# Token groups of 400, 256 and 400, with a joined 512-column matmul for the middle one

## Chip, cores and metric

The kernel runs on one core of a Trainium2 chip. The metric is the device time of one execution in microseconds (us).

## What is computed

One step of a two-layer encoder trunk over 1056 tokens (1024 of a prompt, 32 of a running stream), width 1024, in fp32 accuracy. Layer 0 mixes tokens with a gated width-3 convolution, layer 1 with trailing means over 2, 4, 8 and 16 frames. Each mixer is followed by a squared-ReLU MLP with 4096 hidden features.

```python
def short_conv_mixer(x, hist, w_in, conv_w, w_out):
    gb, gc, h = jnp.split(x @ w_in, 3, axis=-1)
    u = gc * h
    ...
    y = (gb * conv) @ w_out
...
        h = layer_norm(ALPHA * x + y, ln1_g[i], ln1_b[i])
        r = jax.nn.relu(h @ mlp_w1[i])
        f = (r * r) @ mlp_w2[i]
        e = (p[i] @ ple_w[i]) * jax.nn.sigmoid(h @ ple_gate_w[i])
        x = layer_norm(ALPHA * h + f + e, ln2_g[i], ln2_b[i])
```

## The kernel before

Features lie on the 128 partitions and tokens along the free dimension. A feature block is 128 features, so width 1024 is KD = 8 blocks and a group's activations are 8 blocks of TG columns. The 1056 tokens are three groups (n = 0, 1, 2) of TG = 352.

Every matrix product is made in three float32r matmuls. Each value v is split in v_hi, its float32r rounding, and v_lo = v - v_hi; the helper `triple` (lines 612 to 614) sums W_hi x_hi, W_hi x_lo and W_lo x_hi into one PSUM bank. A bank holds 512 fp32 columns per partition, of which 352 are used. Each matmul loads its 128x128 weights first (the PEld rows). A tile of 8 triples is 24 matmuls. The kernel makes 4368 triples: 1456 for each group. Of the 1456, the conv input takes 192, the conv output 64, the gates 128, the MLP's up tiles 512, its down blocks 512, the per-layer embedding ("ple") 32 and the pooling's grouped map 16.

Weights stream from HBM in pieces of 128x1024 (318 of them) through four raw buffers. ScalarE makes the high part (line 717), VectorE the low part (line 545), into one of six slots. ScalarE and VectorE also read the results out of PSUM:

- an **up** step (24 matmuls): ScalarE takes relu from PSUM to `t` (line 831), which frees the bank (`a_free`), squares it (833), rounds it to `r_hi` (837); VectorE makes `r_lo` (1032). Two banks (0, 1) alternate for up and gate tiles.
- a **down** step (24 matmuls in four blocks of 6): VectorE adds each block from PSUM onto `acc` (line 1036) and frees its bank (`b_free`). Four banks (3 to 6) go round.
- a **gate** step: ScalarE takes the sigmoid from PSUM (825), and with the "ple" tile VectorE multiplies and adds (1025, 1027).
- the **conv input** loop: banks 0, 1 and 2 hold gc, h and gb; ScalarE copies gc out (733), VectorE multiplies from the other two (886 to 908).

`make_plan` writes the order of steps out once, and each engine walks the same list in order. The MLP is cut in 16 chunks of two hidden blocks; a visit of a chunk serves group 0 alone first, then 0 and 1, then all three, then 1 and 2, then 2 alone (`LEAD` gives the lengths of the first two parts for each layer). In a visit the up steps of the next group stand before the down steps of the last one. The two hidden blocks of a group's visit lie in one of three `part` buffers of r_hi and r_lo. LayerNorm and pooling work of one group is put beside the steps of the others: `beside` puts each piece on a step where `room`, worked out from the planner's costs (`MM_US`, `ADD_US` and others), leaves VectorE enough time. These pieces stand behind a step's own work on each in-order engine. The last group's final LayerNorm ("finish") stands at the end, alone, with its matrix products in plain fp32 against a matrix of ones (line 641, two matmul instructions for each block).

## Time and profile before

| | |
|---|---|
| median of 3 runs | 2225.42 us (2225.34 to 2225.62) |
| the profiled execution | 2226.73 us, of it 2224.9 us span |
| mean granted TensorE clock | 0.988 of full |
| TensorE busy (matmul) | 2138.0 us, 96% of the span |
| VectorE busy | 1255.6 us, 56% |
| ScalarE busy | 807.8 us, 36% |

The span runs from the first to the last instruction. A matmul's start is recorded, its end is modelled, and successive matmuls overlap in the record (one is listed at about 322 ns, and starts come about every 159 ns), so the cost of a matmul is read from the distance between starts, or from a stretch's length over its count. The clock rows are in tenths of full speed, 2.4 GHz; the other level is 1.2 GHz.

### The profile page before, as it was taken

The numbers are of one execution on the slowest core, as the hardware profiler recorded it, in microseconds if no ns is written. First come the engines' busy times: TensorE is split into PE (matmuls) and PEld (weight loads), VectorE is DVE, ScalarE is ACT, GpSimd is POOL, SyncE is SP. The second block draws the span as 40 slices with busy tenths as digits, with TensorE's granted clock in tenths as the row PEclk, the third lists the DMA queues.
The fourth block names the chain that finished last, engine by engine and source line by source line (L and its number), as shares of the span: only waits on it lengthen the run. The fifth ranks groups of instructions, "written<-read, shape, count | busy, mean of one in ns | idle before, by whom it ended". The sixth has DMA issues, their size and how long they took to land. (4 is left out here: it accounts for less than half of the span.)

```text
span 2224.9 us, 31587 instructions
## 1 busy us (share of the span) xinstructions
PE 2138.0 (96%) x13166; PEld 2119.3 (95%) x13166; DVE 1255.6 (56%) x1823; ACT 807.8 (36%) x1233; POOL 70.3 (3%) x61
## 2 busy tenths in 40 slices
PE   8999999999999999999899999998889999999996
PEld 8999999999999999999889998997889999999996
DVE  4233367785454444435666776876565356445576
ACT  3122123544333222223434454555242234233344
POOL 0000000000000000000200030001000000000000
PEclk9999999999999999999999999999999999999998
DMA  4011142343132111111212343442112211222232
GB/s 166 29 57 42 52 133 64 114 130 124 55 114 67 38 57 39 58 38 39 76 57 76 120 135 103 149 142 69 57 64 87 66 48 56 68 77 76 67 124 98
DMA packets 51455, 179.67 MB, mean 81 GB/s; under 512 B 7936, under 2 KB 8064, under 8 KB 51328
## 3 DMA queue, kind: packets, MB, share of 16 engines
q1 hardware_dynamic: 49248, 177.72, 24.4%
q8 instruction: 95, 1.56, 0.3%
q10 hardware_dynamic: 2080, 0.12, 0.1%
q14 instruction: 32, 0.26, 0.0%
HBM read 173.36 MB, written 4.46 MB: 80 GB/s over the span
## 5 line engine op out<-in xcount | busy, mean ns | idle before, releaser
L612 PE MATMUL ps<-h_hi,w_split 128*128 128x352 f32 x2160 | 704.2, 326 | 30.5 <-ACT y_scaled_t L817 25.0
L614 PE MATMUL ps<-h_hi,w_split 128*128 128x352 f32 x2160 | 696.2, 322 | 0.0
L613 PE MATMUL ps<-h_lo,w_split 128*128 128x352 f32 x2160 | 695.6, 322 | 0.0
L612 PE MATMUL ps<-r_hi,w_split 128*128 128x352 f32 x1632 | 536.3, 329 | 30.3 <-DVE acc L1036 30.3
L614 PE MATMUL ps<-r_hi,w_split 128*128 128x352 f32 x1632 | 527.7, 323 | 0.0
L613 PE MATMUL ps<-r_lo,w_split 128*128 128x352 f32 x1632 | 527.7, 323 | 0.0
L1036 DVE TENSOR_TENSOR acc<-acc,ps 128x352 f32<-128x352 f32 x768 | 377.0, 518 | 146.6 <-PE ps L614 145.4
L612 PEld LDWEIGHTS ps<-h_hi,w_split 128*128 128x128 f32 x2160 | 407.8, 189 | 36.5 <-issue 31.1
L545 DVE TENSOR_TENSOR w_split<-w_raw,w_split 128x1024 fp32r<-128x1024 f32 x294 | 357.0, 1232 | 135.5 <-ACT w_split L717 135.0
L717 ACT CAST w_split<-w_raw 128x1024 fp32r<-128x1024 f32 x294 | 301.4, 1046 | 320.2 <-PE ps L614 319.1
L613 PEld LDWEIGHTS ps<-h_lo,w_split 128*128 128x128 f32 x2160 | 408.9, 189 | 1.1
L614 PEld LDWEIGHTS ps<-h_hi,w_split 128*128 128x128 f32 x2160 | 408.0, 189 | 0.0
L1032 DVE TENSOR_TENSOR r_lo<-t,r_hi 128x352 fp32r<-128x352 f32 x192 | 101.9, 531 | 444.2 <-ACT r_hi L837 444.1
L612 PEld LDWEIGHTS ps<-r_hi,w_split 128*128 128x128 f32 x1632 | 310.3, 190 | 37.3 <-issue 26.8
L613 PEld LDWEIGHTS ps<-r_lo,w_split 128*128 128x128 f32 x1632 | 311.0, 191 | 1.2
L614 PEld LDWEIGHTS ps<-r_hi,w_split 128*128 128x128 f32 x1632 | 309.9, 190 | 0.0
L831 ACT ACTIVATE t<-ps 128x352 f32<-128x352 f32 x192 | 89.0, 463 | 577.1 <-PE ps L614 569.0
L612 PE MATMUL ps<-x_hi,w_split 128*128 128x352 f32 x576 | 187.2, 325 | 9.3 <-DVE w_split L545 9.3
L614 PE MATMUL ps<-x_hi,w_split 128*128 128x352 f32 x576 | 187.3, 325 | 0.0
L613 PE MATMUL ps<-x_lo,w_split 128*128 128x352 f32 x576 | 185.9, 323 | 0.0
L612 PEld LDWEIGHTS ps<-x_hi,w_split 128*128 128x128 f32 x576 | 108.7, 189 | 9.2 <-issue 9.2
L613 PEld LDWEIGHTS ps<-x_lo,w_split 128*128 128x128 f32 x576 | 110.1, 191 | 0.0
(80 smaller groups left out, 1116.1 us busy)
## 6 DMA issues: line engine op xcount, KB each, us to landing
w_raw<-w_stream SPq DMA_DIRECT2D x318, 512.0 KB, 3.4
x_raw<-x_t SPq DMA_DIRECT2D x6, 704.0 KB, 8.2
y_t<-acc SPq DMA_DIRECT2D x4, 704.0 KB, 4.2
w_raw<-p_t SPq DMA_DIRECT2D x6, 352.0 KB, 2.9
y_t<-acc SPq DMA_DIRECT2D x4, 352.0 KB, 2.4
pool_new<-acc ACTq DMA_DIRECT2D x2, 60.0 KB, 6.1
vec<-vectors SPq DMA_DIRECT2D x1, 78.0 KB, 6.9
pool_history<-pool_hist SPq DMA_DIRECT2D x1, 60.0 KB, 6.5
```

The lines of the kernel that those rows point to most:

```text
L545: ins = eng.tensor_tensor(ws[:, slot, 1, :], raw[:, u.q, :], f32(ws[:, slot, 0, :]), ALU.subtract)
L612: pe.matmul(out, wh, mov_h, start=first, stop=False)
L613: pe.matmul(out, wh, mov_l, start=False, stop=False)
L614: return pe.matmul(out, wl, mov_h, start=False, stop=last)
L717: act.copy(ws[:, slot, 0, :], raw[:, u.q, :]).then_inc(w_hi, 1)
L831: act.activation(t, ps[:, step.bank, 0:TG], ACT.Relu).then_inc(a_free, 1)
L1032: dve.tensor_tensor(rpart(rl, *r), tt[:, step.bank, :], f32(rpart(rh, *r)), ALU.subtract).then_inc(r_ready, 1)
L1036: dve.tensor_tensor(blk(acc, step.n, m), blk(acc, step.n, m), ps[:, B_BANK + (step.bank + i) % 4, 0:TG], ALU.add).then_inc(b_free, 1)
```

## The change

The groups become T = (400, 256, 400) columns, beginning at S = (0, 400, 656). Where two copies of a group fit one bank (2T <= 512: `JOINED`, the middle group), `joined` takes the place of `triple`: the first matmul has the weights W_hi and streams x_hi and x_lo together as 512 columns, which land in the two halves of the bank; the second has W_lo and streams x_hi onto the second half alone, 256 columns. What was three matmuls is two, and the result is the sum of the bank's halves. For that x, h and r are each laid out with their high and low parts as one buffer.

VectorE sums the halves: in up and gate steps with one `tensor_reduce` into `t` (`sum_halves`), from which ScalarE then goes on; in the conv input loop with three of them for each m; in down steps with two adds onto `acc`, one from each half, interleaved over the blocks; in conv-output steps with one add more. The "ple" and grouped-map products stay `triple`s, for each group at its own width.

DRAM keeps its layout of three groups of 352, so loads of x and p and stores of y go in pieces (`pieces_of`): groups 0 and 2 take two pieces, of 352 and 48 columns, for each transfer; group 1 takes one. `LEAD` of layer 0 goes from (5, 3) to (5, 4), which makes one more chunk visit with four more weight pieces. Group 1 has a `part` buffer for itself. The planner's costs are given per group.

```diff
--- before.py
+++ after.py
-TAIL = PROMPT - (NG - 1) * TG
+T = (400, 256, 400)
+S = (0, 400, 656)
+TMAX = max(T)
+TAIL = PROMPT - S[-1]
...
-LEAD = (5, 3), (9, 5)
+LEAD = (5, 4), (9, 5)
...
-MM_US, ADD_US, GATE_US, R_LO_US, SPLIT_US = 0.159, 0.52, 0.57, 0.61, 1.23
+MM_US, ADD_US, GATE_US, R_LO_US, SPLIT_US = (0.167, 0.124, 0.167), (0.57, 0.86, 0.57), (0.62, 0.43, 0.62), (0.66, 0.85, 0.66), 1.23
...
+def pieces_of(n):
+
+    out, here = [], 0
+    while here < T[n]:
+        there = S[n] + here
+        width = min(T[n] - here, TG - there % TG)
+        out.append((there // TG, there % TG, here, width))
+        here += width
+    return out
...
-            part = count["part"] % NG
-            count["part"] += 1
+            part = 1 if n == 1 else n if len(todo[v][1]) == NG else 2 - count["part"]
+            if n != 1:
+                count["part"] = part
...
-        own = len(step.refill) * SPLIT_US
+        own, n = len(step.refill) * SPLIT_US, step.n
         if step.kind == "down":
-            return 24 * MM_US - own - 4 * ADD_US
+            return 24 * MM_US[n] - own - 4 * ADD_US[n]
         if step.kind == "up":
-            return 24 * MM_US - own - R_LO_US
+            return 24 * MM_US[n] - own - R_LO_US[n]
         if step.kind == "gate":
-            return 30 * MM_US - own - 2 * GATE_US
-        return 24 * MM_US - own - 2 * ADD_US
+            return 30 * MM_US[n] - own - 2 * GATE_US[n]
+        return 24 * MM_US[n] - own - 2 * ADD_US[n]
 
...
+        def both(t, n, k):
+
+            at = S[n] * KD + k * T[n]
+            return t[:, :, at:at + T[n]]
...
+        def halves(bank, n):
+            return ps[:, bank, 0:T[n]], ps[:, bank, T[n]:2 * T[n]]
...
-                sp.dma_start(half(xraw, n, h), half(x_t, n, h)).then_inc(x_in[n][h], 16)
+                kn = KD // 2
+                for g, there, here, width in pieces_of(n):
+                    sp.dma_start(half(xraw, n, h).rearrange("p (k t) -> p k t", k=kn)[:, :, here:here + width],
+                                 of_dram(x_t, g, h * kn, kn, there, width)).then_inc(x_in[n][h], 16)
...
+            def joined(bank, n, slot, col, mov, mov_h, first, last):
+
+                wh, wl = ws[:, slot, 0, col:col + P], ws[:, slot, 1, col:col + P]
+                pe.matmul(ps[:, bank, 0:2 * T[n]].rearrange("p (a t) -> p a t", a=2), wh, mov, start=first, stop=False)
+                return pe.matmul(halves(bank, n)[1], wl, mov_h, start=False, stop=last)
+
+            def full_tile(bank, slot, src, src_h, src_l, n):
                 for k in range(KD):
-                    mm = triple(ps[:, bank, 0:TG], slot, k * P, blk(src_h, n, k), blk(src_l, n, k), k == 0, k == KD - 1)
+                    if JOINED[n]:
+                        mm = joined(bank, n, slot, k * P, both(src, n, k), blk(src_h, n, k), k == 0, k == KD - 1)
+                    else:
+                        mm = triple(ps[:, bank, 0:T[n]], slot, k * P, blk(src_h, n, k), blk(src_l, n, k), k == 0, k == KD - 1)
                 return mm
...
                         for f in range(CHUNK):
-                            last = triple(ps[:, B_BANK + (step.bank + i) % 4, 0:TG], step.slots[f], m * P, rpart(rh, step.part, f),
-                                          rpart(rl, step.part, f), f == 0, f == CHUNK - 1)
+                            if JOINED[n]:
+                                last = joined(bank, n, step.slots[f], m * P, rboth(step.part, n, f), rpart(rh, step.part, n, f),
+                                              f == 0, f == CHUNK - 1)
+                            else:
+                                last = triple(ps[:, bank, 0:T[n]], step.slots[f], m * P, rpart(rh, step.part, n, f),
+                                              rpart(rl, step.part, n, f), f == 0, f == CHUNK - 1)
                         last.then_inc(b_full, 1)
                 for x in step.side:
                     side(*x)
...
-
-                    wait(act, z_ready, m * 3 + (n - 2))
-                    act.copy(gcs[:, n, :], ps[:, 0, 0:TG]).then_inc(gc_copied, 1)
+                    if not JOINED[n]:
+                        act.wait_ge(gc_full, m * 3 + (n + 1))
+
+                        wait(act, z_ready, m * 3 + (n - 2))
+                        act.copy(gcs[:, n, 0:T[n]], ps[:, 0, 0:T[n]]).then_inc(gc_copied, 1)
...
+            def a_source(step, t):
+
+                if JOINED[step.n]:
+                    act.wait_ge(a_summed, step.summed + 1)
+                    return t
+                act.wait_ge(a_full, step.a + 1)
+                if step.t_free is not None:
+
+                    act.wait_ge(sems[step.t_free[0]], step.t_free[1])
+                return ps[:, step.bank, 0:T[step.n]]
...
+            def add_halves(out, bank, n):
+                return dve.tensor_reduce(out, ps[:, bank, 0:2 * T[n]].rearrange("p (a t) -> p t a", a=2), mybir.AxisListType.X, ALU.add)
...
+                    if JOINED[n]:
+                        dve.wait_ge(gc_full, q1)
+                        add_halves(gcs[:, n, 0:T[n]], 0, n).then_inc(gc_copied, 1)
                     dve.wait_ge(h_full, q1)
                     dve.wait_ge(gc_copied, q1)
-                    at = CH + n * TG
-                    if n < NG - 1:
-                        dve.tensor_tensor(ub[:, at:at + TG], gcs[:, n, :], ps[:, 1, 0:TG], ALU.mult).then_inc(u_done, 1)
+                    if JOINED[n]:
+                        add_halves(ub[:, at:at + T[n]], 1, n).then_inc(h_summed, 1)
+                        dve.wait_ge(h_summed, m + 1)
+                        dve.tensor_tensor(ub[:, at:at + T[n]], gcs[:, n, 0:T[n]], ub[:, at:at + T[n]], ALU.mult).then_inc(u_done, 1)
...
+                    if JOINED[n]:
+                        add_halves(gcs[:, n, 0:T[n]], 2, n).then_inc(gb_summed, 1)
+                        dve.wait_ge(gb_summed, m + 1)
+                        dve.tensor_tensor(gcs[:, n, 0:T[n]], cv[:, n, 0:T[n]], gcs[:, n, 0:T[n]], ALU.mult).then_inc(zf_done, 1)
...
+            def sum_halves(step, t):
+                dve.wait_ge(a_full, step.a + 1)
+                if step.t_free is not None:
+
+                    dve.wait_ge(sems[step.t_free[0]], step.t_free[1])
+                add_halves(t, step.bank, step.n).then_inc(a_summed, 1)
...
+                if step.kind == "gate" and JOINED[step.n]:
+                    sum_halves(step, tt[:, step.bank, 0:T[step.n]])
...
+                    if JOINED[n]:
+                        first.then_inc(out_half, 1)
+                        dve.wait_ge(out_half, step.summed + 1)
+                        first = dve.tensor_tensor(blk(acc, n, m), blk(acc, n, m), halves(i % 2, n)[1], ALU.add)
...
-                    r = (step.part, step.mm)
+                    r, t = (step.part, step.n, step.mm), tt[:, step.bank, 0:T[step.n]]
+                    if JOINED[step.n]:
+                        sum_halves(step, t)
                     dve.wait_ge(r_hi_done, step.t + 1)
-                    dve.tensor_tensor(rpart(rl, *r), tt[:, step.bank, :], f32(rpart(rh, *r)), ALU.subtract).then_inc(r_ready, 1)
+                    dve.tensor_tensor(rpart(rl, *r), t, f32(rpart(rh, *r)), ALU.subtract).then_inc(r_ready, 1)
+                elif step.kind == "down" and JOINED[step.n]:
+                    last = len(step.blocks) - 1
+                    for i, m in enumerate(step.blocks):
+                        dve.wait_ge(b_full, step.b + (i + 1))
+                        a = halves(B_BANK + (step.bank + i) % 4, step.n)[0]
+                        dve.tensor_tensor(blk(acc, step.n, m), blk(acc, step.n, m), a, ALU.add).then_inc(b_half, 1)
+                        for j in ((i - 1,) if i < last else (i - 1, i)):
+                            if j >= 0:
+                                dve.wait_ge(b_half, step.half + (j + 1))
+                                b, mj = halves(B_BANK + (step.bank + j) % 4, step.n)[1], step.blocks[j]
+                                dve.tensor_tensor(blk(acc, step.n, mj), blk(acc, step.n, mj), b, ALU.add).then_inc(b_free, 1)
                 elif step.kind == "down":
                     for i, m in enumerate(step.blocks):
```

## Rows read from the trace of the kernel before

**Rows 1.** Page: the span, busy time, and busy tenths in 40 slices.

```profile
span 2224.9 us, 31587 instructions
...
PE 2138.0 (96%) x13166; PEld 2119.3 (95%) x13166; DVE 1255.6 (56%) x1823; ACT 807.8 (36%) x1233; POOL 70.3 (3%) x61
...
PE   8999999999999999999899999998889999999996
...
DVE  4233367785454444435666776876565356445576
```

**Rows 2.** Stretches (us): time, busy of each engine, granted clock, DMA share, GB/s.

```profile
600.00:1000.00 400.00, 400.00 (x2520) 400.00 (x2519) 173.79 (x294) 114.77 (x195) 0.00 (x0) 1.00 0.18 59
1045.00:1690.00 645.00, 594.76 (x3581) 584.78 (x3581) 444.74 (x603) 285.66 (x439) 50.99 (x30) 0.97 0.28 91
2200.50:2224.90 24.40, 7.60 (x20) 4.10 (x18) 13.66 (x25) 8.69 (x17) 0.00 (x0) 0.72 0.15 59
```

**Rows 3.** Timeline, full clock: start us, took us, engine, line, operation.

```profile
999.97 0.32 PE L612 MATMUL ps<-r_hi,w_split 128*128 128x352 f32 x1
...
1000.92 0.32 PE L612 MATMUL ps<-r_hi,w_split 128*128 128x352 f32 x1
```

**Rows 4.** Timeline, half clock, first tile: start us, took us.

```profile
10.87 0.50 PE L614 MATMUL ps<-x_hi,w_split 128*128 128x352 f32 x1
...
12.04 0.49 PE L612 MATMUL ps<-x_hi,w_split 128*128 128x352 f32 x1
12.05 0.33 PEld L613 LDWEIGHTS ps<-x_lo,w_split 128*128 128x128 f32 x1
```

**Rows 5.** Timeline after an idle TensorE, full clock: start us, took us.

```profile
1033.90 0.19 PEld L612 LDWEIGHTS ps<-r_hi,w_split 128*128 128x128 f32 x1 [1.53 <-issue]
...
1034.33 0.19 PEld L612 LDWEIGHTS ps<-r_hi,w_split 128*128 128x128 f32 x1
```

**Rows 6.** Timeline after an idle TensorE, half clock.

```profile
1106.00 0.29 PEld L612 LDWEIGHTS ps<-h_hi,w_split 128*128 128x128 f32 x1 [5.87 <-issue]
```

**Rows 7.** Weight loads of the plain-fp32 matmuls: half clock, then full.

```profile
2205.60 0.34 PEld L641 LDWEIGHTS ps<-ln_squares,ones 128*128 128x128 f32 x1 [0.25 <-ACT ln_squares L757]
...
2207.36 0.34 PEld L641 LDWEIGHTS ps<-ln_squares,ones 128*128 128x128 f32 x1 [0.25 <-issue]
...
2208.29 2.56 PEld L641 LDWEIGHTS ps<-ln_squares,ones 128*128 128x128 f32 x9
```

**Rows 8.** Groups by line and shape: busy us, mean ns, idle before.

```profile
L1036 DVE TENSOR_TENSOR acc<-acc,ps 128x352 f32<-128x352 f32 x768 | 377.0, 518 | 146.6 <-PE ps L614 145.4
...
L1032 DVE TENSOR_TENSOR r_lo<-t,r_hi 128x352 fp32r<-128x352 f32 x192 | 101.9, 531 | 444.2 <-ACT r_hi L837 444.1
...
L973 DVE TENSOR_TENSOR acc<-acc,rstd 128x2816 f32<-128x2816 f32 x11 | 33.9, 3086 | 0.0
...
L965 DVE RECIPROCAL std<-std 128x352 f32<-128x352 f32 x12 | 28.2, 2347 | 0.6 <-ACT std L770 0.6
...
L890 DVE TENSOR_TENSOR u<-gc,ps 128x320 f32<-128x320 f32 x8 | 3.9, 490 | 46.5 <-PE ps L614 46.5
...
L891 DVE TENSOR_TENSOR u<-gc,ps 128x32 f32<-128x32 f32 x8 | 1.4, 180 | 0.0
```

**Rows 9.** Timeline, VectorE: adds back to back.

```profile
999.77 1.40 DVE L1036 TENSOR_TENSOR acc<-acc,ps 128x352 f32<-128x352 f32 x3
```

**Rows 10.** Waits of TensorE: us in total, times, longest.

```profile
PE ps L612 <- DVE acc L1036: 30.3, 17, 5.5
PE ps L612 <- ACT y_scaled_t L817: 25.0, 11, 5.7
PE ps L612 <- DVE w_split L545: 10.0, 2, 9.3
```

**Rows 11.** Page, DMA issues: count, KB each, us to landing.

```profile
x_raw<-x_t SPq DMA_DIRECT2D x6, 704.0 KB, 8.2
```

More of the change, by code:

```diff
@@ L78 @@
     t_free: object = None
+    summed: int = 0
+    half: int = 0
     r_used: int = 0
@@ L155, in make_plan @@
     stays = []
-    count = {"out": 0, "a": 0, "b": 0, "t": 0, "gate": 0, "part": 0}
+    count = {"out": 0, "a": 0, "b": 0, "t": 0, "gate": 0, "part": 0, "summed": 0, "half": 0, "b_half": 0}
     t_free, r_used, held = [None, None], {}, {}
@@ L177, in token_inputs @@
     def token_inputs(layer, n):
-        part = min(range(NG), key=lambda part: r_used.get(part, 0))
+        part = min((part for part in range(NG) if T[part] >= T[n]), key=lambda part: r_used.get(part, 0))
         held[n] = part
@@ L190, in outs @@
                     count["out"] += 1
-                    use(add("out", n=n, m=4 * half + mm, a=count["out"] - 1), units[mm])
+                    use(add("out", n=n, m=4 * half + mm, a=count["out"] - 1, summed=count["half"]), units[mm])
+                    count["half"] += JOINED[n]
     def gates(layer, n):
@@ L204, in gates @@
             a = count["a"]
-            step = add("gate", layer=layer, n=n, m=m, a=a, bank=a % 2, t_free=t_free[a % 2])
+            step = add("gate", layer=layer, n=n, m=m, a=a, bank=a % 2, t_free=t_free[a % 2], summed=count["summed"])
+            count["summed"] += JOINED[n]
             use(step, stay(("gate", layer, m)))
@@ L227, in ups @@
                 a, t = count["a"], count["t"]
-                step = add("up", n=n, part=part, mm=mm, a=a, bank=a % 2, t=t, r_used=r_used.get(part, 0), t_free=t_free[a % 2])
+                step = add("up", n=n, part=part, mm=mm, a=a, bank=a % 2, t=t, r_used=r_used.get(part, 0), t_free=t_free[a % 2],
+                           summed=count["summed"])
+                count["summed"] += JOINED[n]
                 use(step, up_units[v][mm])
@@ L237, in downs @@
             for blocks in (range(0, 4), range(4, 8)):
-                step = add("down", n=n, part=part, blocks=blocks, b=count["b"], bank=count["b"] % 4, r_need=ready)
+                step = add("down", n=n, part=part, blocks=blocks, b=count["b"], bank=count["b"] % 4, r_need=ready, half=count["b_half"])
+                count["b_half"] += len(blocks) * JOINED[n]
                 use(step, *down_units[v])
@@ L566, in x_load @@
             def x_load(n, h):
-                sp.dma_start(half(xraw, n, h), half(x_t, n, h)).then_inc(x_in[n][h], 16)
+                kn = KD // 2
+                for g, there, here, width in pieces_of(n):
+                    sp.dma_start(half(xraw, n, h).rearrange("p (k t) -> p k t", k=kn)[:, :, here:here + width],
+                                 of_dram(x_t, g, h * kn, kn, there, width)).then_inc(x_in[n][h], 16)
             x_load(0, 0)
@@ L596, in _ @@
                     sp.wait_ge(affine, (len(NORMS) - NG + n) * 2 + h + 1)
-                    sp.dma_start(half(y_t, n, h), half(acc, n, h)).then_inc(out_done, 16)
+                    kn = KD // 2
+                    for g, there, here, width in pieces_of(n):
+                        sp.dma_start(of_dram(y_t, g, h * kn, kn, there, width),
+                                     half(acc, n, h).rearrange("p (k t) -> p k t", k=kn)[:, :, here:here + width]).then_inc(out_done, 16)
             for k in range(0, KD, 2):
                 sp.wait_ge(last_affine, k + 2)
-                cols = slice((NG - 1) * GCOLS + k * TG, (NG - 1) * GCOLS + (k + 2) * TG)
-                sp.dma_start(y_t[:, cols], acc[:, cols]).then_inc(out_done, 16)
-            sp.wait_ge(out_done, 16 * (2 * (NG - 1) + KD // 2 + 1))
+                for g, there, here, width in pieces_of(NG - 1):
+                    sp.dma_start(of_dram(y_t, g, k, 2, there, width), grp3(acc, NG - 1)[:, k:k + 2, here:here + width]).then_inc(out_done, 16)
+            stores = [2 * len(pieces_of(n)) for n in range(NG - 1)] + [KD // 2 * len(pieces_of(NG - 1))]
+            sp.wait_ge(out_done, 16 * (sum(stores) + 1))
             sp.wait_ge(state_out, 32)
@@ L640, in side @@
                         pe.wait_ge(last_squared, k + 1)
-                        last = pe.matmul(ps[:, GRP_BANK, 0:TG], ones[:], blk(squares, n, k), start=k == 0, stop=k == KD - 1)
+                        last = pe.matmul(ps[:, GRP_BANK, 0:T[n]], ones[:], blk(squares, n, k), start=k == 0, stop=k == KD - 1)
                     last.then_inc(var_full, 1)
@@ L646, in side @@
                     wait(pe, var_copied, i)
-                    pe.matmul(ps[:, LN_BANK, 0:TG], ones[:], s_mean[:], start=True, stop=True).then_inc(mean_full, 1)
+                    width = T[NORMS[i][2]]
+                    pe.matmul(ps[:, LN_BANK, 0:width], ones[:], s_mean[:, 0:width], start=True, stop=True).then_inc(mean_full, 1)
                 elif what == "var":
@@ L650, in side @@
                     pe.wait_ge(centred, i + 1)
-                    pe.matmul(ps[:, LN_BANK, 0:TG], ones[:], s_var[:], start=True, stop=True).then_inc(var_full, 1)
+                    width = T[NORMS[i][2]]
+                    pe.matmul(ps[:, LN_BANK, 0:width], ones[:], s_var[:, 0:width], start=True, stop=True).then_inc(var_full, 1)
                 elif what == "grp":
```

218 lines of the change are left out of this document (115 added, 103 removed).

## The prediction

> **What bounds the kernel now.** I read the page first: TensorE is busy 96% of the span, VectorE 56%, and in the 40 slices TensorE falls under 9 only early on and in the second half, where VectorE stands at 6 to 8 tenths [rows 1]. So TensorE's stream of matmuls sets the time, and there are two questions: what one matmul costs, and where the stream breaks.
>
> The cost comes from a quiet stretch. From 600 to 1000 us 2520 matmuls start in 400 us at full clock [rows 2]: 158.7 ns each; six starts in a row give (1000.92 - 999.97) / 6 = 158 [rows 3]. 352 columns at 2.4 GHz are 146.7 ns, so 12.0 ns are not streaming. Either every matmul carries a constant of 12 ns, or something else sets a floor near 159 ns, under which 352 columns hide. The change is worth something by the second reading and nothing by the first, so this is the point to settle. Three readings speak for a floor:
>
> - At half clock the distance is (12.04 - 10.87) / 4 = 293 ns [rows 4], just 352 / 1.2. No constant is left.
> - The plain-fp32 matmuls pass 352 columns twice in an instruction: (2207.36 - 2205.60) / 3 = 587 ns at half clock, and (2.56 - 0.19) / 8 = 296 at full clock [rows 7], against 293.3 for 704 columns. Where streaming is long, 2 to 3 ns are left, not 12; I take 2.5.
> - The weight load is 0.19 us at full clock whether TensorE stood idle before it or was streaming [rows 5]: the stream does not lengthen it. At half clock it is 0.29 after an idle stretch [rows 6] and 0.33 while streaming [rows 4, 7], so there it does wait for the stream. At full clock 352 columns are over before the next weights are in.
>
> So I take a matmul as the longer of 158.7 ns and N/2.4 + 2.5 ns.
>
> The breaks: in 1045 to 1690 us 3581 matmuls take 645 us [rows 2], where 158.7 ns each would be 568.3, so 77 us are lost there, to waits and to half clock after them. The waits are for VectorE's adds from the down banks (30.3 us) and for the pooling's scaled tile (25.0) [rows 10]: LayerNorm and pooling pieces stand in VectorE's queue before what TensorE needs. Outside that stretch and the two ends little is lost.
>
> **The change part by part.**
>
> Groups 0 and 2: 2 x 1456 x 3 = 8736 matmuls go from 352 to 400 columns, 158.7 to 169.2 ns: +10.5 each, +91.7 us.
>
> Group 1: of its 1456 triples 1408 are joined (all but 32 "ple" and 16 grouped-map ones). Three at 158.7 are 476.1 ns; 512 columns are 215.8 and 256 columns the floor, 158.7: 374.5. That is -101.6 x 1408 = -143.1 us. The 144 other matmuls, at 256 columns, stay on the floor: 0. Sum **-51.4 us**.
>
> Bounds. Below: without the 2.5 ns it is 8736 x 8.0 = +69.9 and 1408 x (476.1 - 372.0) = -146.6, so -76.7. Above, with the 12 ns as a constant: 400 columns 178.7, 512 and 256 together 344.0, so +174.7 - 186.0 - 5.8 (the 144) = -17.1. Furthest above, each column at 158.7 / 352 = 0.451 ns and the floor as well: 180.3 and 230.8 + 158.7, +188.7 - 121.9 = +67; I put little on it, since the long fp32 matmuls of [rows 7] stream at the clock's rate. The two-run operand of the joined matmul is in no row; I price it as one run.
>
> The Trainium skill (TensorE: Matmul & The Clock Gate, "Back-to-back issue gap") gives N/2.4 + 2.5 ns for an isolated warm matmul. At 352 columns that is 149.2 against 158.7 in [rows 2], and the measurement decides; at 704 columns it is 295.8 against 296 in [rows 7]. By that rule alone at all widths the change would give 8736 x 20.0 - 1408 x 122.6 - 144 x 40 = -3.7 us in place of -51.4.
>
> VectorE's new work. Adds back to back come every (1.40 - 0.52) / 2 = 0.44 us [rows 9], and width costs (490 - 180) / 288 = 1.08 ns a column by L890 and L891 in [rows 8]. A group-1 block of two 256-wide adds: 2 x 0.337 = 0.674, +0.234 x 256 blocks = +60 us. The 512 wider blocks of the others: +0.052 each, +26. The reduction over two halves is in no row: at one element a cycle it is 0.490 + 192 x 0.00108 = 0.70; if it went by outputs it would be 0.42 (256 columns); the dearest VectorE row is the reciprocal, 2.35 for 352 [rows 8], the far bound. I take 0.70, nearest in kind (reads from PSUM). 64 up steps: + (0.70 - 0.10 saved on r_lo), +38; the other ups +7; gates, conv input (three for each m) and outputs about +20. Together some +150 us, so VectorE goes to about 1400 us, 64%.
>
> The Trainium skill (VectorE: DVE Perf Modes, "The perf-mode tier table") lists tensor_reduce as having only the 1x mode, and its rules call it the slowest VectorE operation. No run here shows one yet; 1x is my 0.70.
>
> Is it hidden? In group 1's down steps a block takes TensorE 2 x 374.5 = 749 ns and VectorE 674: it keeps pace, but catches up by only 0.075 a block, where it had 0.952 - 0.44 = 0.51. A LayerNorm pass takes 3.09 us at 2816 columns by L973 in [rows 8], and will take 3.49 for the 400 groups and 2.29 for the 256 one. The four banks cover 4 x 0.952 = 3.8 us now, 4.06 beside 400-column downs, but 3.0 beside group 1's. So in quiet stretches the adds and the sums hide behind matmuls (VectorE 174 of 400 us there [rows 2]), and where LayerNorm and pooling run the waits grow. In an up step of group 1 ScalarE, and with it `a_free`, now stands behind VectorE's queue; the bank is wanted again only a tile later (8 x 374.5 = 3.0 us). 44 of the 150 us fall in the lossy stretch (645 of 2225 us), where VectorE is busy 445 [rows 2]. Bounds 0 and 44; I take 0.3 of it, **+13 us**: most of VectorE's idle time is waiting for ScalarE's r_hi (444 us in all by L1032 in [rows 8]) and can't be used. The `LEAD` step's four more splits add some 5 us to VectorE and hide in the quiet part.
>
> Start: TensorE's first wait is 9.3 us for the first split [rows 10], behind x's first piece. 800 KB for 704 at 8.2 us to landing [rows 11] is +1.1, casts wider by an eighth +0.2: **+1.3**. The 48-column runs of 192 bytes could make it 3.
>
> Tail: 24.4 us from the last down block [rows 2], in which VectorE is busy 13.7 and TensorE 7.6, mostly in turn; I take some 18 in series that go with group 2's width: x 48/352 = **+2.5**; the doubled stores could add 1.
>
> Sum: -51.4 + 13 + 1.3 + 2.5 = -34.6. The profiled execution would go from 2226.7 to 2192.1; the median of the runs, 1.3 us lower, to **2191**.
>
> **The rivals.**
>
> *A constant per matmul, no floor* (0.12). For it: 12 ns on each. Against: the half clock and the fp32 rows. -17.1 + 16.8 = 0: 2225. The skill's rule alone gives -3.7 + 16.8, 2238; that belongs here, with 0.03 of the 0.12, since [rows 2] contradicts it at 352 columns.
>
> *VectorE becomes the bound* (0.18), the side that is slower. [...] If half of the 150 us becomes waiting: -51.4 + 75 + 3.8 = +27: 2253. It decides against the change once waits grow by more than 47.6 us. [...] Against: the pieces are placed by per-group costs, and group 1's own passes get shorter.
>
> *More than forecast* (0.08): nothing over the clock's rate and no new waits: -76.7 + 3.8 = -73: 2153.
>
> **How the numbers follow.** The forecast case has 0.62; its own range is 2172 to 2216, with waits from 0 to about 40 us. Over all cases 2155 to 2240 leaves out half of the "more" case (0.04) and the worse half of VectorE's (0.09). A measurement here tells 0.2%, 4.5 us, from no change. Faster: 0.61 of the forecast case, 0.08, 0.03 of the constant and 0.02 of VectorE: 0.74; same 0.08 (0.06 of the constant, the rest between); slower 0.18.
>
> **What would show it.** Starts 169 ns apart in groups 0 and 2, and 216 + 159 in group 1; a distance of 119 after the 256-column matmul would mean the constant. The sum of halves at 0.70 us. TensorE's waits for VectorE at 30 + 13 us; above 80 VectorE has won. First matmul about 1 us later, tail about 27 us. The prediction is wrong above all if the joined matmul costs more than 216 ns, or the waits grow by more than 40.

## The result, and the profile after

The changed kernel takes 2329.04 us (median of 4, 2327.93 to 2336.38) where the kernel before takes 2225.38: a ratio of 1.0473, 95% interval 1.0452 to 1.0495. It is 104 us slower. I had forecast 2191, with 2240 as the top of the range. The profiled execution took 2336.4 us, 2334.6 of it span.

The page of the changed kernel, its span, busy time and 40 slices, beside [rows 1]:

```profile
span 2334.6 us, 29173 instructions
...
PE 2186.8 (94%) x11758; PEld 2090.3 (90%) x11758; DVE 1409.7 (60%) x2195; ACT 814.7 (35%) x1231; POOL 68.9 (3%) x61
...
PE   8999998998999999998889989996888998999996
...
DVE  4433466676564454557767865776577457655676
```

TensorE issues 11758 matmuls in place of 13166 and yet is busy 49 us longer. Its row falls under 9 early, in the middle and late, in many more slices than before. VectorE is at 1410 us, close to the 1400 that I had forecast.

The stream first. Two starts from the changed kernel's timeline, in a tile of triples at 400 columns (start, took):

```profile
1850.16 0.34 PE L663 MATMUL ps<-h_hi_lo,w_split 128*128 128x400 f32 x1
...
1851.80 0.35 PE L663 MATMUL ps<-h_hi_lo,w_split 128*128 128x400 f32 x1
```

The second is the ninth start after the first: (1851.80 - 1850.16) / 9 = 182.2 ns. I had put 169.2. Now a joined down step (L670 is the 512-column matmul, L671 the 256-column one):

```profile
817.12 0.40 PE L670 MATMUL ps<-r_hi_lo,w_split 128*128 128x512 f32 x1
817.36 0.28 PE L671 MATMUL ps<-r_hi_lo,w_split 128*128 128x256 f32 x1
817.47 0.40 PE L670 MATMUL ps<-r_hi_lo,w_split 128*128 128x512 f32 x1
...
819.24 0.40 PE L670 MATMUL ps<-r_hi_lo,w_split 128*128 128x512 f32 x1
819.48 0.28 PE L671 MATMUL ps<-r_hi_lo,w_split 128*128 128x256 f32 x1
820.36 0.47 PE L670 MATMUL ps<-r_hi_lo,w_split 128*128 128x512 f32 x1 [0.61 <-DVE acc L1150]
```

The pair takes (819.24 - 817.12) / 6 = 353.3 ns, where 374.5 was forecast: within it 512 columns take 240 ns, not 216, and 256 take 110, not 159. There is no floor at 159, and wide matmuls cost more than N/2.4 + 2.5 ns. By these distances the stream changed by 8736 x (182.2 - 158.7) = +205, 1408 x (353.3 - 476.1) = -173 and 144 x (119 - 158.7) = -6 us: **+27 us**, where I had -51.4.

Then the waits of TensorE in the changed kernel (total, times, longest), beside [rows 10]:

```profile
PE ps L663 <- DVE acc L1154: 33.7, 16, 5.3
PE ps L663 <- ACT y_scaled_t L888: 29.9, 12, 6.4
PE ps L670 <- DVE acc L1150: 25.2, 30, 3.3
...
PE ps L670 <- ACT t L904: 9.2, 8, 3.9
PE ps L663 <- ACT t L904: 5.6, 2, 4.1
PE ps L663 <- DVE acc L1115: 4.3, 1, 4.3
```

All of TensorE's listed waits add up to 133.0 us, before to 73.3: **+60 us**. New are L1150, the second add of a joined block, and the waits for ScalarE's sigmoid (L904) and relu (L907), which before came to 0.3 us. The mean granted clock is 0.976 (before 0.988): the clock stands at half for 2 x 0.024 x 2334.6 = 112 us, before for 53. In the traces 260 of the stream's matmuls start at half clock, before 123. Priced by their distances at the two levels (400 columns 333 and 182 ns, 352 columns 293 and 159, a joined pair 640 and 353), that is an estimated 38 us against 16: **+21**. The three parts make 108 of the span's 110 us. Two stretches of the changed kernel, beside [rows 2], show where:

```profile
600.00:1000.00 400.00, 393.04 (x2162) 376.95 (x2161) 204.50 (x381) 113.94 (x191) 0.00 (x0) 1.00 0.18 60
...
1600.00:1800.00 200.00, 165.55 (x836) 153.18 (x836) 137.18 (x220) 77.77 (x129) 18.48 (x10) 0.93 0.21 66
```

The quiet stretch is not quiet any longer: TensorE is idle 7 us of 400 there. And in the pooling stretch of layer 1 it is busy 166 of 200, at 0.93 of the clock.

The costs on VectorE, by group and shape (busy, mean ns, idle before), beside [rows 8]:

```profile
L1154 DVE TENSOR_TENSOR acc<-acc,ps 128x400 f32<-128x400 f32 x512 | 278.0, 568 | 119.5 <-PE ps L665 117.8
...
L1145 DVE TENSOR_TENSOR acc<-acc,ps 128x256 f32<-128x256 f32 x256 | 101.8, 418 | 2.9 <-PE ps L671 2.5
L1150 DVE TENSOR_TENSOR acc<-acc,ps 128x256 f32<-128x256 f32 x256 | 101.4, 418 | 0.0
...
L941 DVE TENSOR_REDUCE t<-ps 128x256 f32<-128x512 f32 x80 | 55.0, 688 | 18.3 <-PE ps L671 17.0
...
L1064 DVE TENSOR_TENSOR acc<-acc,rstd 128x3200 f32<-128x3200 f32 x7 | 24.4, 3485 | 0.0
```

568 ns at 400 columns, 418 at 256, 688 for the sum of halves (0.70 forecast) and 3485 for a LayerNorm pass (3.49 forecast): these were right.

### The profile page after: what moved, and what is told of

It reads as the page before. It is cut to its first block and busy times, and to the rows that moved or that the text cites. A ratio compares the mean times of both kernels' runs of the same rounds, so it can differ in the third digit from the quotient of the medians.

```text
span 2334.6 us, 29173 instructions
## 1 busy us (share of the span) xinstructions
PE 2186.8 (94%) x11758; PEld 2090.3 (90%) x11758; DVE 1409.7 (60%) x2195; ACT 814.7 (35%) x1231; POOL 68.9 (3%) x61
## 5 line engine op out<-in xcount | busy, mean ns | idle before, releaser
L663 PE MATMUL ps<-h_hi_lo,w_split 128*128 128x400 f32 x1456 | 507.9, 349 | 42.1 <-ACT y_scaled_t L888 29.9
L665 PE MATMUL ps<-h_hi_lo,w_split 128*128 128x400 f32 x1456 | 507.7, 349 | 0.0
L664 PE MATMUL ps<-h_hi_lo,w_split 128*128 128x400 f32 x1456 | 507.7, 349 | 0.0
L663 PE MATMUL ps<-r_hi_lo,w_split 128*128 128x400 f32 (+1 forms) x1120 | 393.3, 351 | 33.8 <-DVE acc L1154 33.7
L664 PE MATMUL ps<-r_hi_lo,w_split 128*128 128x400 f32 (+1 forms) x1120 | 391.1, 349 | 0.0
L665 PE MATMUL ps<-r_hi_lo,w_split 128*128 128x400 f32 (+1 forms) x1120 | 390.7, 349 | 0.0
L1154 DVE TENSOR_TENSOR acc<-acc,ps 128x400 f32<-128x400 f32 x512 | 278.0, 568 | 119.5 <-PE ps L665 117.8
L1139 DVE TENSOR_TENSOR r_hi_lo<-t,r_hi_lo 128x400 fp32r<-128x400 f32 (+1 forms) x192 | 103.4, 539 | 397.7 <-ACT r_hi_lo L913 397.5
L663 PEld LDWEIGHTS ps<-h_hi_lo,w_split 128*128 128x128 f32 x1456 | 278.0, 191 | 47.8 <-issue 41.8
L665 PEld LDWEIGHTS ps<-h_hi_lo,w_split 128*128 128x128 f32 x1456 | 279.7, 192 | 0.1
L664 PEld LDWEIGHTS ps<-h_hi_lo,w_split 128*128 128x128 f32 x1456 | 277.9, 191 | 0.8
L670 PE MATMUL ps<-h_hi_lo,w_split 128*128 128x512 f32 x704 | 259.4, 409 | 15.8 <-ACT t L904 9.2
L663 PEld LDWEIGHTS ps<-r_hi_lo,w_split 128*128 128x128 f32 x1120 | 215.6, 193 | 42.5 <-DVE r_hi_lo L1139 31.8
L664 PEld LDWEIGHTS ps<-r_hi_lo,w_split 128*128 128x128 f32 x1120 | 215.5, 192 | 1.4 <-issue 0.3
L665 PEld LDWEIGHTS ps<-r_hi_lo,w_split 128*128 128x128 f32 x1120 | 215.3, 192 | 0.1
L907 ACT ACTIVATE t<-ps 128x400 f32<-128x400 f32 x128 | 64.4, 503 | 419.1 <-PE ps L665 417.6
L670 PE MATMUL ps<-r_hi_lo,w_split 128*128 128x512 f32 x512 | 186.7, 405 | 25.2 <-DVE acc L1150 25.2
L671 PE MATMUL ps<-h_hi_lo,w_split 128*128 128x256 f32 x704 | 200.4, 285 | 0.0
L670 PEld LDWEIGHTS ps<-h_hi_lo,w_split 128*128 128x128 f32 x704 | 135.9, 193 | 50.6 <-issue 14.3
L670 PEld LDWEIGHTS ps<-r_hi_lo,w_split 128*128 128x128 f32 x512 | 97.2, 190 | 54.4 <-issue 33.8
```

The source lines that it names most:

```text
L663: pe.matmul(out, wh, mov_h, start=first, stop=False)
L664: pe.matmul(out, wh, mov_l, start=False, stop=False)
L665: return pe.matmul(out, wl, mov_h, start=False, stop=last)
L670: pe.matmul(ps[:, bank, 0:2 * T[n]].rearrange("p (a t) -> p a t", a=2), wh, mov, start=first, stop=False)
L671: return pe.matmul(halves(bank, n)[1], wl, mov_h, start=False, stop=last)
L907: act.activation(t, a_source(step, t), ACT.Relu).then_inc(a_free, 1)
```

## The experiments

Each ran beside the kernel before on the same chip, and the ratios are to that.

### Which part makes the loss

**e1_unjoined**: the changed kernel with its groups and its order of steps, but no joined matmuls.

```diff
-JOINED = tuple(2 * t <= 512 for t in T)
+JOINED = (False, False, False)
```

> Groups of 400, 256 and 400 as in the change, but group 1 keeps its triples at 256 columns; the order of steps is the same. After the change 256 columns took 117 ns and 512 took 237, so three matmuls of 256 are 351 ns against 353 joined: TensorE's stream loses 3 us and no more. VectorE loses the 104 sums of halves and 256 second adds, some 120 us. Theory 1, the joining makes the new waits (VectorE's second adds and sums in the way of TensorE): the time falls by 40 to 70 us, to 2260 to 2290. Theory 2, the group sizes make them (group 1's down blocks last 0.70 us, so four banks cover 2.8 us, less than ScalarE's three passes over 400 columns for which VectorE waits first): the time stays within 15 us of 2329.

Measured: 2261.73 us, ratio 1.0145 (1.0107 to 1.0184). Theory 1 holds. Joining costs 1.0473 - 1.0145 = 3.3%, some 73 us. What it gains on TensorE's stream is small, for a joined triple passes the same 768 columns (512 + 256) as three matmuls of 256: three at 120 ns are 360 against 353.3, some 9 us in all. TensorE's waits are back at 72.3 us; three kinds of them:

```profile
PE ps L663 <- ACT y_scaled_t L888: 23.0, 12, 6.4
PE ps L663 <- DVE acc L1154: 15.8, 12, 3.1
...
PE ps L663 <- ACT t L904: 7.0, 3, 3.3
```

Without a second add the L1150 waits are gone, and the wider groups' down blocks wait 16 us, not 34. The block time of group 1 is the same as when joined (6 x 0.12 = 0.72 us, against 0.71), so theory 2, that short blocks alone exhaust the four banks, falls.

**e2_equal**: the changed kernel with three equal groups.

```diff
-T = (400, 256, 400)
-S = (0, 400, 656)
+T = (352, 352, 352)
+S = (0, 352, 704)
...
-MM_US, ADD_US, GATE_US, R_LO_US, SPLIT_US = (0.167, 0.124, 0.167), (0.57, 0.86, 0.57), (0.62, 0.43, 0.62), (0.66, 0.85, 0.66), 1.23
+MM_US, ADD_US, GATE_US, R_LO_US, SPLIT_US = (0.159,) * 3, (0.52,) * 3, (0.57,) * 3, (0.61,) * 3, 1.23
...
-        part = min((part for part in range(NG) if T[part] >= T[n]), key=lambda part: r_used.get(part, 0))
+        part = min((part for part in range(NG) if n == 1 or part != 1), key=lambda part: r_used.get(part, 0))
```

> The changed kernel with three groups of 352 (nothing joined), the planner's old costs, and all else as changed: the longer LEAD, the part buffer of its own for group 1, the combined high and low buffers. Theory 1 and 2 both put the whole loss on the groups of 400, 256 and 400: 2225, within 8 us. The rival, that the longer LEAD or the fixed part buffers cost time: 2240 or more.

Measured: 2221.64 us, ratio 0.9963 (0.9939 to 0.9987). So the longer `LEAD`, the part buffers and the combined buffers together lose nothing, and are even a little under before (what each does alone was not run). The unequal groups with nothing joined are 1.8% over this (e1), about 40 us.

**e5_join_downs** and **e6_join_tiles**: `JOINED` split in two flags, one for the down blocks, one for all other tiles.

```diff
-JOINED = tuple(2 * t <= 512 for t in T)
+JOINED = (False, False, False)
+JOINED_DOWN = tuple(2 * t <= 512 for t in T)
...
-                count["b_half"] += len(blocks) * JOINED[n]
+                count["b_half"] += len(blocks) * JOINED_DOWN[n]
...
-                elif step.kind == "down" and JOINED[step.n]:
+                elif step.kind == "down" and JOINED_DOWN[step.n]:
```

(TensorE's down step tests `JOINED_DOWN` too. e6 has the two values the other way round.)

> The changed kernel with only group 1's down blocks joined; its gate, up, conv-input and conv-output tiles are triples of 256 columns, so VectorE sums no halves there. Nothing joined was 2262, all joined 2329. Joining a triple is worth 362 - 354 = 8 ns of stream, so about 4 us here. If the second add in each down block makes the waits (1.5 times the adds, while the banks of a 0.70 us block run out): 2300 to 2325. If ScalarE's relu and sigmoid waiting behind VectorE's sums makes them: 2255 to 2275.

> The opposite half: group 1's gate, up, conv-input and conv-output tiles joined, its down blocks triples of 256 columns. Stream about 8 us less than with nothing joined. If the second adds in down blocks make the waits: 2252 to 2270. If the sums of halves do: 2300 to 2320. If each makes its part, this run and the other together lose about the 67 us that lie between 2262 and 2329.

Measured: downs alone 2280.86 us, ratio 1.0247 (1.0232 to 1.0263); tiles alone 2306.18, ratio 1.0351 (1.0329 to 1.0373). Over e1 that is +1.0 and +2.1%, together 3.1 of the 3.3%, as forecast for the case that each makes its part. The downs alone lie between the two ranges given for them; the tiles alone lie in the range of the sums of halves, which have the larger part. TensorE's waits with the downs alone joined, two rows:

```profile
PE ps L671 <- DVE acc L1151: 24.7, 30, 3.3
PE ps L664 <- DVE acc L1155: 10.7, 7, 4.6
```

and with the tiles alone joined, three:

```profile
PE ps L664 <- DVE acc L1155: 38.5, 21, 5.2
PE ps L664 <- ACT y_scaled_t L889: 26.6, 12, 6.4
...
PE ps L671 <- ACT t L905: 9.2, 8, 3.9
```

The L1151 row (L1150 in the changed kernel) comes whole with the joined downs: 30 times, 24.7 us. The sums of halves do their harm elsewhere: the waits for ScalarE's sigmoid (L905) are 14.9 us in all, where e1 has 7.0, and the triples' waits for VectorE's down adds (L1155) 38.5, where e1 has 15.8. The mean granted clock fell to 0.978 with the tiles joined (e1 0.985) and was 0.988 with the downs.

### How VectorE's order makes the waits

The changed kernel's timeline at one of the stops, in the joined down step shown above (ScalarE and VectorE):

```profile
816.98 0.50 ACT L907 ACTIVATE t<-ps 128x400 f32<-128x400 f32 x1 [1.78 <-PE ps L665]
...
818.09 0.53 ACT L913 CAST r_hi_lo<-t 128x400 fp32r<-128x400 f32 x1
...
818.65 0.58 DVE L1139 TENSOR_TENSOR r_hi_lo<-t,r_hi_lo 128x400 fp32r<-128x400 f32 x1 [2.19 <-ACT r_hi_lo L913]
...
819.14 0.75 DVE L1145 TENSOR_TENSOR acc<-acc,ps 128x256 f32<-128x256 f32 x2
...
819.80 0.41 DVE L1150 TENSOR_TENSOR acc<-acc,ps 128x256 f32<-128x256 f32 x1
```

The last up tile of group 2 is complete about 816.95. ScalarE makes relu, square and r_hi, to 818.6. VectorE stands behind that in its queue (idle 2.19 us before 818.65), makes r_lo, and only then begins on group 1's blocks, of which TensorE has by then finished three. A block's bank is free after three adds, since the second add of block 0 stands behind the first one of block 1: the first L1150 ends at 820.21, and TensorE, whose four banks were full at about 819.6, goes on at 820.36. With one add for each block the first bank would have been free some 0.7 us sooner, by an estimate from these rows (the first add would end at 819.14 + 0.42 = 819.56).

**e4_defer**: the changed kernel with r_lo of a group's second up tile made later, inside the next down step.

```diff
+    for step, after in zip(plan, plan[1:]):
+        step.late = step.kind == "up" and step.mm == CHUNK - 1 and after.kind == "down"
...
+            late = []
+
+            def r_low(step):
+                r, t = (step.part, step.n, step.mm), tt[:, step.bank, 0:T[step.n]]
+                dve.wait_ge(r_hi_done, step.t + 1)
+                dve.tensor_tensor(rpart(rl, *r), t, f32(rpart(rh, *r)), ALU.subtract).then_inc(r_ready, 1)
...
+                    if step.late:
+                        late.append(step)
+                    else:
+                        r_low(step)
...
+                        if i == 2 and late:
+                            r_low(late.pop())
```

(In a down step of the other groups it follows the second block, `i == 1`.)

> The changed kernel, but VectorE's r_lo of a group's second up tile is made after the next down step's first two or three blocks are added, not before them. If VectorE's wait for ScalarE's passes over the up tile is what fills the four banks in group 1's down steps, the stop of 0.77 us at each visit's second down step goes, and others shrink: 20 to 40 us less, 2290 to 2310. If VectorE's amount of work is the cause: no change, within 8 us of 2329.

Measured: 2283.73 us, ratio 1.0243 (1.0204 to 1.0283), 2.3% under the changed kernel and some 45 us, more than the 20 to 40 expected, with VectorE as busy as before the edit (1418 us). So with the amount of its work unchanged another order takes back nearly half of the loss. Four rows of TensorE's waits:

```profile
PE ps L667 <- ACT y_scaled_t L892: 31.9, 12, 6.4
PE ps L667 <- DVE acc L1169: 15.5, 8, 4.0
...
PE ps L674 <- ACT t L908: 9.4, 8, 3.9
...
PE ps L674 <- DVE acc L1163: 4.3, 2, 3.3
```

The waits for the second add (now L1163) are 4.3 us in 2 times, not 25.2 in 30, and those for the wider blocks 15.5, not 33.7. The sigmoid's and the pooling's waits hardly change.

**e8_unjoined_defer**: nothing joined, and the late r_lo.

> Groups of 400, 256 and 400, nothing joined, and the late r_lo. If the order on VectorE makes group 1's waits whatever the load, the late r_lo is worth here what it is with equal groups (25 us): 2262 - 25 = about 2237, leaving only the stream's longer 400-column matmuls (some 25 us) over the 2200 of equal groups. If it is worth 45 us as with all joined: about 2217. If the waits were gone with the joining: 2255 or more.

Measured: 2255.22 us, ratio 1.0116 (1.0084 to 1.0148). That is 6 us under e1, with intervals that overlap. The expectations of 2237 and 2217 missed, and the third case, 2255 or more, came: where nothing is joined the late r_lo has little to take away (e1's waits for adds were 22 us in all, and are 17 here). So in the changed kernel neither the order alone nor the added work alone makes the loss that e4 took back, but the two together. What is left over equal groups with the same edit (below, 2200 to 2204) is some 50 us: the stream's +36 (8736 x 23.5 - 4368 x 38.7 ns, with 120 ns for 256 columns) and TensorE's waits, 12 us longer than in f2 (72.7 us against 60.4). Those for ScalarE's sigmoid and relu are 11.2 us against 0.9, and those for the adds of the conv output 6.3 against 2.1; group 1's short tiles (24 x 0.12 = 2.9 us) leave less time for both.

### What a column costs

**e3_columns** and **e7_columns2**: the kernel before, with rows of matmuls added after its last output block is ready, when the other engines have nothing left to do. Their results are not used.

```diff
             walk(plan, do)
+            pe.wait_ge(last_affine, KD)
+
+            def series(count, out, weights, moving):
+                for i in range(count):
+                    pe.matmul(out, weights(i), moving(i), start=True, stop=True)
...
+            for bank, n in enumerate((64, 128, 256, 352, 400, 512)):
+                series(24, ps[:, 1 + bank, 0:n], w_r, one_run(n))
+            series(24, ps[:, 0, 0:512].rearrange("p (a t) -> p a t", a=2), w_r, two_runs)
```

> The kernel before with rows of float32r matmuls at its end, all other engines idle: 24 each of 64, 128, 256, 352, 400 and 512 columns, 24 of 512 columns as two runs of 256, and 12 plain-fp32 ones of 352 and of 256. Their results are not used. Theory, float32r columns stream at 0.45 ns each at full clock: 117, 159, 182 and 232 ns at 256, 352, 400 and 512, and the two runs at 236. Rival 1, the other engines' traffic slows the stream: with them idle 0.417 a column, 147 ns at 352. Rival 2, a weight load sets a floor: the same distance for 64, 128 and perhaps 256 columns, above 107 ns. The two-run operand costs more than the one run by 5 ns or more if the joined form has a price of its own.

> The kernel before with further rows of matmuls at its end, results unused: float32r of 256 and 512 columns at half clock; of 16, 192 and 224 columns at full clock; 352 and 400 columns with weights and operands in the kernel's own order (W_hi, W_hi, W_lo on blocks that lie 352 or 400 columns apart); 352 with one and the same weights; and 2-byte operands of 256, 352 and 512 columns. The first such run gave N/2.4 + 13.3 ns for float32r and a least distance of 111.7. Theory, a constant of 13.3 ns in the float32r form at full clock: 192 and 224 columns at 112 (floor) and 107 to 112, 16 at 112, half clock 213 and 427, and the 2-byte ones at N/2.4 + 2.5: 109 (or the floor), 149 and 216. Rival, the constant belongs to any matmul that loads new weights: 2-byte ones at 120, 160 and 227 too. Whether the 182.5 ns of 400 columns in the kernel (180 in the first such run) come from the placing of the blocks: then 182 to 183 here, else 180.

Two readings of the same series each, merged by the timeline, give a distance: (length - length) / (count - count). First float32r at 256 columns:

```profile
2230.30 0.93 PE L709 MATMUL ps<-h_hi,w_split 128*128 128x256 f32 x6
...
2230.30 2.97 PE L709 MATMUL ps<-h_hi,w_split 128*128 128x256 f32 x23
```

(2.97 - 0.93) / (23 - 6) = 120 ns. Then 2-byte operands at 256 columns:

```profile
2266.74 0.93 PE L709 MATMUL ps<-h_hi,w_split 128*128 128x256 bf16 x7
...
2266.74 2.35 PE L709 MATMUL ps<-h_hi,w_split 128*128 128x256 bf16 x20
```

(2.35 - 0.93) / (20 - 7) = 109 ns. The distances from start to start of all series, as the traces record them (means within a series, ns):

```
columns                        16     64    128    192    224    256    352    400    512  2x256
float32r, full clock        111.7  111.7  111.7      -  111.5  120.0  160.0  180.3  226.9  226.7
float32r, half clock            -      -      -    213      -    213    293      -    427      -
2-byte, full clock              -      -      -      -      -  109.1  149.1      -  215.8      -
plain fp32, full clock          -      -      -      -      -  215.8  295.8      -      -      -
float32r, kernel's order        -      -      -      -      -      -  158.8  182.2      -      -
```

(The float32r row at full clock is from e3, but for 16 and 224 columns. In e7, on another chip, the same series of 352 columns took 161.1, so 1 ns can lie between runs.) From 256 columns on, float32r takes N/2.4 + 13.3 ns, to within 1 ns: 120.0, 160.0, 180.0, 226.6. Each further column is at the clock's rate, and 13 ns are a constant. 2-byte operands and plain fp32 (with 2N columns passed) have 2.5 in its place. At half clock the constant is not there (293 = 352 / 1.2). The floor that I had taken for the cause is real but lies at 111.7 ns, and at 213 at half clock: 224 columns and fewer hide under it at full clock, 192 at half. The two-run operand costs nothing more than one run in these series. So the theory of 0.45 ns a column fell as well: two points, 117 and 183, happened to lie on such a line. Expectations on idle engines (147 at 352) and on new weights (2-byte at 120, 160 and 227) were wrong too. The kernel's own order at 400 columns takes 182.2 with all other engines idle (e7), the same as in the changed kernel, so the other engines' traffic is not what puts it above the 180.3 of e3. In e3 the operands begin at multiples of 2048 bytes. At 352 columns the kernel's order takes 158.8, against 160.0 in e3 and 161.1 in e7 with starts at such multiples, and one and the same weights take 161.0 in e7. That speaks for the placing of the blocks, worth about 2 ns either way; for 400 columns the two placings were not run side by side. The joined pair stays unexplained: by the series 226.9 + 120.0 = 346.9 ns, in the kernel 353.3.

What makes the constant, the runs don't show; only that it goes with the float32r form and with full clock.

### A version that beats both

**f1_defer_before**: the kernel before, with e4's edit alone. **f2_equal_defer**: e2 with it.

> The kernel before (groups of 352) with the one edit that took 45 us off the changed kernel: r_lo of a group's second up tile is made after two blocks of the next down step are added. Here a block lasts 0.96 us and four banks cover 3.8 us, so only the waits beside LayerNorm and pooling can shrink (30 us for VectorE's adds). If these come from the same order: 2215 to 2222 where before is 2228. If they come from LayerNorm's passes alone: no difference beyond 3 us.

> Equal groups in the changed kernel's code with the longer LEAD (0.4% faster than before on the last chip) and the late r_lo as well. If the two gains add: 8 to 20 us under before. If the late r_lo gives nothing with equal groups: 0.4% again, and no difference from the run without it.

Measured: f1 2200.15 us, ratio 0.9892 (0.9874 to 0.991); f2 2203.51, ratio 0.9904 (0.9886 to 0.9922). Both beat both kernels, f1 by 1.1%, and both by more than expected (26 and 23 us under before); what e2 had gained does not add. The page of f1, beside [rows 1]:

```profile
span 2195.5 us, 31587 instructions
...
PE 2120.4 (97%) x13166; PEld 2103.2 (96%) x13166; DVE 1265.4 (58%) x1823; ACT 808.0 (37%) x1233; POOL 70.7 (3%) x61
```

TensorE's waits, beside [rows 10]:

```profile
PE ps L616 <- ACT y_scaled_t L821: 25.0, 10, 6.9
PE ps L616 <- DVE acc L1048: 17.5, 16, 2.4
```

and VectorE's:

```profile
DVE acc L1048 <- PE ps L618: 287.8, 460, 3.7
DVE r_lo L1020 <- ACT r_hi L841: 245.9, 78, 4.9
```

VectorE waited 444 us for r_hi [rows 8] and now 246. It spends the difference waiting for TensorE's blocks, 288 us against 146, which is the wait that costs nothing. TensorE's waits for its adds fall from 30.3 to 17.5 us, and the mean clock rises from 0.988 to 0.994: 2 x 0.006 x 2195.5 = 26 us at half clock, where it was 53. All listed waits together fall from 73.3 to 61.4 us, and 49 matmuls in place of 123 start at half clock, by the estimate above some 10 us less. That is 22 of the 29 us between the two spans; the rest was not taken apart.

**f4_defer_spaced**: f1 with the pooling's grouped map one step later.

```diff
-                rows.append((1, 1.1, [("grp", 8 * n + 2 * q - 2 + j, 4 + (q - 1) // 2) for j in range(2)]
+                rows.append((2, 1.1, [("grp", 8 * n + 2 * q - 2 + j, 4 + (q - 1) // 2) for j in range(2)]
...
-        rows.append((2, 1.1, [("grp", 8 * n + 6 + j, 5) for j in range(2)] + [("gadd", 8 * n + 6 + j) for j in range(2)]))
+        rows.append((3, 1.1, [("grp", 8 * n + 6 + j, 5) for j in range(2)] + [("gadd", 8 * n + 6 + j) for j in range(2)]))
```

> The kernel before with the late r_lo, and the pooling's grouped map placed one step later behind its centring. TensorE still waits 25 us for the pooling's scaled tile, since the map's matmuls stand in its order before window sums and centring are done. If that is a matter of place: 8 to 20 us under the 2200 of the late r_lo alone. If the later map pushes the LayerNorm behind it into the next waits: no gain, or up to 10 us more.

Measured: 2203.26 us, ratio 0.9879 (0.9854 to 0.9905), no difference from f1: the second case. TensorE's waits:

```profile
PE ps L616 <- DVE acc L1048: 23.6, 18, 4.2
PE ps L616 <- ACT y_scaled_t L821: 16.8, 12, 3.1
```

The pooling's wait fell from 25.0 to 16.8 us and the adds' rose from 17.5 to 23.6: the wait moved.

## Why the prediction was wrong

**The step that failed** is "So I take a matmul as the longer of 158.7 ns and N/2.4 + 2.5 ns". The cost is N/2.4 + 13.3 ns from 256 columns on, with a floor at 111.7. The stream changed by +27 us, not -51.4. Of my two readings the constant was right, and I had it as a rival with 0.12. Its 2225 for the whole kernel was still 104 too low. Each of the three supports was a sound reading of something else:

- No constant at half clock [rows 4]: true, also in e7. It shows that the constant is hidden there, not that it is missing at full clock.
- 2.5 ns on the plain-fp32 matmuls [rows 7]: true (295.8 in e3). But float32r is another form, and its constant is its own. I carried a number from one form to another. The Trainium skill (TensorE: Matmul & The Clock Gate, "Back-to-back issue gap") gives N/2.4 + 2.5 ns for the isolated warm matmul. The 2-byte and plain-fp32 series agree with that to 0.1 ns, and float32r doesn't.
- The weight load's equal length with and without a stream [rows 5]: there is a floor of the loads, at 111.7 ns. That it is not the 158.7 could have been seen in the same stretch of the trace, where the load after that of 1033.90 [rows 5] starts only 0.11 us behind it:

```profile
1034.01 0.19 PEld L613 LDWEIGHTS ps<-r_lo,w_split 128*128 128x128 f32 x1
```

The terms: groups 0 and 2 cost +205 us, not +91.7. The joined triples gave -173, not -143. With 13.3 ns in place of 2.5 and the floor at 111.7, the prediction's own sum would have been -2 us: +186 for the 400-column matmuls, -182 for the joined triples, -6 for the rest. So the constant accounts for 50 of the 78 us by which the stream was off. The other 29 are distances in the kernel that lie above the series: 2.2 ns at 400 columns (19 us; perhaps the blocks' placing) and 6.7 ns a joined pair (9 us; open). The bound "furthest above", +67, was the only one that held the measured +27; that was luck, since its 0.451 ns a column and its floor at 158.7 are both wrong.

**The waits** were the second step, off by 47 us: +13 forecast, with 44 as the upper bound, and +60 measured, with an estimated 21 more of matmuls at half clock, for which the prediction had no term of its own. What failed is the bound itself: I took it from VectorE's added busy time in the lossy stretch. In VectorE's in-order queue what delays TensorE is all that stands before the adds, idle time included, above all that behind ScalarE's r_hi. I had called that time unusable, and did not ask who waits during it. "It keeps pace, but catches up by only 0.075 a block" compared two rates, and left out that VectorE starts on group 1's blocks when three of them are done, and that the first bank comes free only after three adds. e4 shows it: the same busy time, 2.3% less. "In quiet stretches the adds and the sums hide behind matmuls" was wrong too: TensorE idles 7 of 400 us there. (The 3.49 us of a LayerNorm pass was right, though the 1.08 ns a column of the same paragraph would make it 3.50.)

**The rival "VectorE becomes the bound"** named the right side and gave 2253. The waits did grow by more than its 47.6 us, but it did not decide alone: with the stream at +27 the change loses even with no new wait. It was half right on what happens. VectorE's work does hold TensorE up (L1154 33.7 us), but e4 takes 18 of these away by order alone, and VectorE is busy only 60% of the span. What I named as the sign, waits for VectorE above 80 us where 30 were for its adds before, did not come as stated: the waits for its adds (L1154, L1150, L1115, L1120) make 66, and 85 only with those for ScalarE's relu and sigmoid, which in group 1 stand behind VectorE's sums.

**Right**: VectorE's prices (0.67 a joined block, 0.69 a sum, 3.49 a pass), that the two-run operand has no price in the series (e3; whether it has a part in the pair's 6 ns is open), that the start hardly matters (the first wait is 10.3 us for 9.3), that the `LEAD` step costs nothing (e2, together with the buffers).

**Which part of the 104 us is from what**: joining some 73 us (e1), of it 23 with the downs and 46 with the other tiles (e5, e6); the unequal groups with nothing joined some 40 over equal ones (e1, e2), of which some 36 are the stream; less the 8 us of e2. The 46 us of the tiles can be divided by the traces of e6 and e1: TensorE's waits grow by 37 us (of these 23 for the triples' down adds, L1155, and 8 for ScalarE's sigmoid and relu), 244 matmuls in place of 164 start at half clock (an estimated 14 us), and the joined stream gives back 6.

## What to carry to other kernels

Price a matmul from rows of its own form, at two widths at least: one width can't tell a constant from a floor, and another type's constant is not this one's. On an in-order engine ask what it waits for just before the work that frees a buffer. Moving that wait behind two or three adds was worth 1.1% in the kernel before, 2.3% in the changed one and 0.3%, within the noise, in the one with unequal groups and nothing joined, while moving the pooling's map only moved a wait. Before joining matmuls, count the columns that pass: here they stayed the same, the busiest engine won 9 us in all, and the second instruction between a result and its bank's release cost far more than that.

## What the hardware showed that I had not expected

- float32r matmuls take N/2.4 + 13.3 ns from start to start at full clock (256 to 512 columns), where 2-byte and plain-fp32 ones take 2.5 over their columns. At half clock they take N/1.2 (e3, e7).
- The least distance of float32r matmuls, each with its weight load, is 111.7 ns at full clock, the same at 16, 64 and 128 columns. At half clock 192 columns take 213 ns, as 256 do.
- In the kernel's order, with blocks 1600 bytes apart, 400 columns take 182.2 ns (e7 and the changed kernel); with blocks that begin at multiples of 2048 bytes 180.3 (e3, another run).
- A moving operand of two runs of 256 columns costs what one of 512 does in a series (226.7 and 226.9, e3). In the joined pair, followed by a 256-column matmul, the two together take 353.3 ns, 6 more than the series add up to.
